# Three 256-column matmuls per weight tile into one PSUM region, and ScalarE as the first reader of PSUM

## What is computed

```
h      = rms_norm(x) * (1 + scale) + shift          # scale, shift, gate: c_act @ mod_w + mod_b
x      = x + gate * mixer(h)                        # attention or Hyena: matmuls with w_in and w_out
h      = rms_norm(x) * (1 + scale2) + shift2
x      = x + gate2 * (square(relu(h @ w1)) @ w2)
```

## Time and profile before

| | |
|---|---|
| median of 3 runs | 2755.25 us (2755.12 to 2758.21) |
| profiled execution, span | 2753.4 us, 41866 instructions |
| HBM read | 597.41 MB, 221 GB/s over the span |
| PE matmuls and weight loads | 13492 each |

### The profile page before, as it was taken

The page is one execution under the profiler, slowest core; times in us unless marked ns, Lnnn a source line. Parts: engine busy times, 40 slices in busy tenths (PEclk is TensorE's granted clock), DMA queues, the critical chain, the costliest instruction groups (busy, mean ns, idle before and its releaser), DMA issues.

```text
span 2753.4 us, 41866 instructions
## 1 busy us (share of the span) xinstructions
PE 2537.7 (92%) x13492; PEld 2107.1 (77%) x13492; DVE 2000.8 (73%) x2357; ACT 1120.8 (41%) x1494; POOL 84.5 (3%) x35
## 2 busy tenths in 40 slices
PE   7879986688999999999989999998899999999996
PEld 2338873376888888888868788787688888888885
DVE  7788658866877878878768788877665555565554
ACT  2234214543444444444434324233344444444442
POOL 0000015500000000000000000000000000000000
PEclk9989988899999999999989999999899999999998
DMA  8858845475888888888848557566466666666662
GB/s 314 321 174 276 285 153 161 160 234 171 271 278 277 282 275 283 276 281 283 277 158 277 195 194 267 175 229 221 153 183 185 188 184 186 187 183 185 188 181 94
DMA packets 441691, 608.73 MB, mean 221 GB/s; under 512 B 18363, under 2 KB 387228, under 8 KB 439580
## 3 DMA queue, kind: packets, MB, share of 16 engines
q1 hardware_dynamic: 440188, 598.53, 66.1%
q10 hardware_dynamic: 1440, 9.44, 0.9%
HBM read 597.41 MB, written 10.49 MB: 221 GB/s over the span
## 4 chain that ended last, share of the span: by engine, by line
PE 84%; DVE 10%; issue 2%; ACT 2%; DMA 1%; DVEq 0%; ACTq 0%; SPq 0%
PE ps L365 49%; PE ps L367 25%; PE ps L1120 2%; PE ps L665 1%; DVE w_lo L397 1%; PE ps L1130 1%; PE ps L937 1%; DMA raw<-in_mod_w 1%; DVE hm L717 1%; DVE hm L725 1%; PE ps L901 1%; DVE sm L1537 1%; DVE lat L731 1%; DVE sm L1534 1%; DVE acc L409 1%
## 5 line engine op out<-in xcount | busy, mean ns | idle before, releaser
L397 DVE TENSOR_TENSOR w_lo<-raw,w_hi 128x1024 fp32r<-128x1024 f32 x720 | 878.5, 1224 | 546.6 <-ACT w_hi L393 542.5
L365 PE MATMUL ps<-lat,w_hi 128*128 128x512 f32 x3200 | 1148.6, 401 | 62.2 <-DVE lat L731 57.0
L393 ACT ACTIVATE w_hi<-raw 128x1024 fp32r<-128x1024 f32 x720 | 760.5, 1060 | 1060.1 <-PE ps L367 987.3
L365 PE MATMUL ps<-alt,w_hi 128*128 128x512 f32 x2688 | 958.9, 400 | 8.5 <-DVE mod L421 5.7
L367 PE MATMUL ps<-lat,w_lo 128*128 128x256 f32 x3200 | 905.9, 283 | 0.0
L365 PEld LDWEIGHTS ps<-lat,w_hi 128*128 128x128 f32 x3200 | 609.8, 191 | 210.2 <-issue 68.4
L367 PE MATMUL ps<-alt,w_lo 128*128 128x256 f32 x2688 | 755.2, 281 | 0.0
L367 PEld LDWEIGHTS ps<-lat,w_lo 128*128 128x128 f32 x3200 | 615.3, 192 | 0.2
L365 PEld LDWEIGHTS ps<-alt,w_hi 128*128 128x128 f32 x2688 | 507.3, 189 | 132.5 <-DVE mod L421 6.0
L367 PEld LDWEIGHTS ps<-alt,w_lo 128*128 128x128 f32 x2688 | 510.1, 190 | 0.3
L409 DVE SCALAR_TENSOR_TENSOR acc<-slab,silu,acc 128x1024 f32<-128x1024 f32 x285 | 367.5, 1293 | 6.1 <-DMA slab<-in_mod_w 2.8
(11 more groups left out here) (185 smaller groups left out, 1519.3 us busy)
## 6 DMA issues: line engine op xcount, KB each, us to landing
raw<-in_mlp_w SPq DMA_DIRECT2D x512, 512.0 KB, 3.7
slab<-in_mod_w SPq DMA_DIRECT2D x336, 512.0 KB, 5.7
raw<-in_hy_w_in SPq DMA_DIRECT2D x96, 512.0 KB, 6.0
raw<-in_mod_w SPq DMA_DIRECT2D x48, 512.0 KB, 6.5
raw<-in_attn_w_in SPq DMA_DIRECT2D x48, 512.0 KB, 6.1
raw<-in_attn_w_out SPq DMA_DIRECT2D x32, 512.0 KB, 5.6
raw<-in_hy_w_out SPq DMA_DIRECT2D x32, 512.0 KB, 5.8
spec_dram<-spec ACTq DMA_DIRECT2D x8, 1024.0 KB, 7.9
```

Source lines behind the costliest of these rows:

```text
L365: e.matmul(ps[:, bank, :], w_hi[:, n % RING, kk, cols], t[:, kb, :], start=(kb == 0), stop=False)
L393: e.activation(w_hi[:, n % RING], raw[:, n % RING], ACT.Copy).then_inc(hi_ready, 1)
L397: e.tensor_tensor(w_lo[:, n % RING], raw[:, n % RING], w_hi[:, n % RING].bitcast(F32), ALU.subtract).then_inc(split_ready, 1)
```

## The change

The two products with `w_hi` become two matmuls of 256 columns, and all three of a tile add into the same 256 columns of PSUM. The halves fb=0 and fb=1 share a bank: g=0 uses bank 0, g=1 bank 1 (the context banks 4 and 5). The first matmul in the bank alone has start set. PSUM then holds the finished sum, so one engine reads it: ACT, with the scale, bias, gate or relu in the same instruction, and then gives `psum_free`. DVE's additions of `lo_sum` go; `lo_sum` and `lo_copied` are removed, and one buffer `gated` [128, 2, 256] serves both g. Readouts:

- `Queries`, `KeysValues`: ACT writes q, keys and values directly; DVE does nothing.
- `Gated`: ACT writes gate times PSUM to `gated`, after a wait on `x_added` for DVE's addition before; DVE does one addition to x.
- `Hidden`: ACT does relu to `sum_sb`, DVE one multiplication.
- `ShortConv`: ACT writes `sum_sb` with its bias; DVE's addition goes.

`act_stats` waits for `x_added`. Two waits of PE ahead of work in other banks grow: `pe_finish` after the output projection waits for the reads of both g, and so does `invert(0, 0)` in the Hyena layer.

```diff
                     kb = (n % 4) * UNIT_KB + kk
                     for fb in range(2):
                         cols = slice(fb * P, (fb + 1) * P)
-                        for t, bank in ((tile, 2 * g + fb), (ctx_tile, 4 + 2 * g + fb)):
+                        for t, bank in ((tile, g), (ctx_tile, 4 + g)):
                             if t is None:
                                 continue
-                            e.matmul(ps[:, bank, :], w_hi[:, n % RING, kk, cols], t[:, kb, :],
-                                     start=(kb == 0), stop=False)
-                            mm = e.matmul(ps[:, bank, 0:TOK], w_lo[:, n % RING, kk, cols], t[:, kb, 0:TOK],
-                                          start=False, stop=(kb == KB - 1))
+                            out = ps[:, bank, fb * TOK:(fb + 1) * TOK]
+                            first, last = (kb == 0 and fb == 0), (kb == KB - 1 and fb == 1)
+                            e.matmul(out, w_hi[:, n % RING, kk, cols], t[:, kb, 0:TOK],
+                                     start=first, stop=False, skip_group_check=True)
+                            e.matmul(out, w_hi[:, n % RING, kk, cols], t[:, kb, TOK:2 * TOK],
+                                     start=False, stop=False, skip_group_check=True)
+                            mm = e.matmul(out, w_lo[:, n % RING, kk, cols], t[:, kb, 0:TOK],
+                                          start=False, stop=last, skip_group_check=True)
                 mm.then_inc(units_done, 1)
         def pe_call(e, T, n, tile, ready, k=None):
...
-            def bank(self, g, part):
-                return ps[:, 2 * g:2 * g + 2, part * TOK:(part + 1) * TOK]
+            def bank(self, g):
+                return ps[:, g, :].rearrange("p (f t) -> p f t", f=2)
             def act_wait(self, e, T, g):
                 e.wait_ge(units_done, 8 * T + 4 * g + 4)
                 e.wait_ge(psum_free, 2 * T + g - 1)
-            def act_head(self, e, T, g):
-                self.act_wait(e, T, g)
-                e.activation(lo_sum[:, g], self.bank(g, 1), ACT.Copy).then_inc(lo_copied, 1)
-
             def act_tail(self, e, T, g):
+                pass
+
+            def dve_head(self, e, T, g):
                 pass
             def dve_tail(self, e, T, g):
...
             def act_head(self, e, T, g):
                 self.act_wait(e, T, g)
-                e.activation(lo_sum[:, g], self.bank(g, 1), ACT.Copy, scale=QSCALE).then_inc(lo_copied, 1)
-
-            def dve_head(self, e, T, g):
-                e.wait_ge(lo_copied, 2 * T + g + 1)
-                e.scalar_tensor_tensor(q[:, ds(4 * self.i + 2 * g, 2), :], self.bank(g, 0), QSCALE, lo_sum[:, g],
-                                       ALU.mult, ALU.add).then_inc(psum_free, 1)
+                e.activation(q[:, ds(4 * self.i + 2 * g, 2), :], self.bank(g), ACT.Copy, scale=QSCALE).then_inc(psum_free, 1)
         class KeysValues(Readout):
             def __init__(self, dst):
                 self.dst = dst
-            def ctx_bank(self, g, part):
-                return ps[:, 4 + 2 * g:6 + 2 * g, part * TOK:(part + 1) * TOK]
-
             def act_head(self, e, T, g):
                 self.act_wait(e, T, g)
-                e.activation(lo_sum[:, g], self.bank(g, 1), ACT.Copy)
-                e.activation(sum_sb[:, g], self.ctx_bank(g, 1), ACT.Copy).then_inc(lo_copied, 1)
-
-            def dve_head(self, e, T, g):
-                e.wait_ge(lo_copied, 2 * T + g + 1)
                 d = self.dst[:, 2 * g:2 * g + 2, :]
-                e.tensor_tensor(d[:, :, 0:TOK], self.bank(g, 0), lo_sum[:, g], ALU.add)
-                e.tensor_tensor(d[:, :, TOK:2 * TOK], self.ctx_bank(g, 0), sum_sb[:, g],
-                                ALU.add).then_inc(psum_free, 1)
+                e.activation(d[:, :, 0:TOK], self.bank(g), ACT.Copy)
+                e.activation(d[:, :, TOK:2 * TOK], self.bank(4 + g), ACT.Copy).then_inc(psum_free, 1)
         class Gated(Readout):
...
             def act_head(self, e, T, g):
                 self.act_wait(e, T, g)
                 e.wait_ge(mod_ready, self.ready)
+
+                e.wait_ge(x_added, self.n_out + 2 * self.i + g)
                 for fb in range(2):
                     f = 4 * self.i + 2 * g + fb
                     bias = gate_bias[:, ds(f, 1)] if self.bias else 0.0
-                    ins = e.activation(lo_sum[:, g, fb], ps[:, 2 * g + fb, TOK:2 * TOK], ACT.Identity,
+                    ins = e.activation(gated[:, fb], ps[:, g, fb * TOK:(fb + 1) * TOK], ACT.Identity,
                                        bias=bias, scale=mod[:, ds(self.gate + f, 1)])
-                ins.then_inc(lo_copied, 1)
+                ins.then_inc(psum_free, 1)
             def dve_head(self, e, T, g):
-                e.wait_ge(lo_copied, 2 * T + g + 1)
-                for fb in range(2):
-                    f = 4 * self.i + 2 * g + fb
-                    xf = x[:, ds(f, 1), :]
-                    ins = e.scalar_tensor_tensor(xf, ps[:, 2 * g + fb:2 * g + fb + 1, 0:TOK],
-                                                 mod[:, ds(self.gate + f, 1)], xf, ALU.mult, ALU.add)
-                ins.then_inc(x_hi_added, 1)
-                e.wait_ge(x_hi_added, self.n_out + 2 * self.i + g + 1)
+                e.wait_ge(psum_free, 2 * T + g + 1)
                 xg = x[:, ds(4 * self.i + 2 * g, 2), :]
-                e.tensor_tensor(xg, xg, lo_sum[:, g], ALU.add).then_inc(psum_free, 1)
+                e.tensor_tensor(xg, xg, gated[:], ALU.add).then_inc(x_added, 1)
         class Hidden(Readout):
...
             def __init__(self, i, n_hid):
                 self.i, self.n = i, n_hid
+            def act_head(self, e, T, g):
+                self.act_wait(e, T, g)
+                e.activation(sum_sb[:, g], self.bank(g), ACT.Relu).then_inc(psum_free, 1)
+
             def dve_head(self, e, T, g):
-                e.wait_ge(lo_copied, 2 * T + g + 1)
-                e.tensor_tensor(sum_sb[:, g], self.bank(g, 0), lo_sum[:, g], ALU.add).then_inc(psum_free, 1)
                 e.wait_ge(psum_free, 2 * T + g + 1)
-                e.scalar_tensor_tensor(sum_sb[:, g], sum_sb[:, g], 0.0, sum_sb[:, g],
-                                       ALU.max, ALU.mult).then_inc(squared, 1)
+                e.tensor_tensor(sum_sb[:, g], sum_sb[:, g], sum_sb[:, g], ALU.mult).then_inc(squared, 1)
             def act_tail(self, e, T, g):
                 e.wait_ge(squared, self.n + 2 * self.i + g + 1)
...
             def act_head(self, e, T, g):
                 self.act_wait(e, T, g)
                 for fb in range(2):
-                    ins = e.activation(lo_sum[:, g, fb], ps[:, 2 * g + fb, TOK:2 * TOK], ACT.Identity,
+                    ins = e.activation(sum_sb[:, g, fb], ps[:, g, fb * TOK:(fb + 1) * TOK], ACT.Identity,
                                        bias=vec("b_in", self.col + 2 * g + fb))
-                ins.then_inc(lo_copied, 1)
-
-            def dve_head(self, e, T, g):
-                e.wait_ge(lo_copied, 2 * T + g + 1)
-                e.tensor_tensor(sum_sb[:, g], self.bank(g, 0), lo_sum[:, g], ALU.add).then_inc(psum_free, 1)
+                ins.then_inc(psum_free, 1)
             def act_tail(self, e, T, g):
                 e.wait_ge(psum_free, 2 * T + g + 1)
...
-        def act_stats(e, k, c, T):
-
-            e.wait_ge(psum_free, 2 * T + 2)
+        def act_stats(e, k, c):
+
+            e.wait_ge(x_added, X_FROM[k] + 2 * c + 2)
             e.wait_ge(square_sums, 4 * k + c)
             e.activation(sq[:, 0], x[:, ds(4 * c, 4), :], ACT.Square).then_inc(squares, 1)
...
             e.wait_ge(mod_ready, FIN_ATT + 2)
             pe_call(e, T_OUT, 4, alt, lambda i: lambda j: (head_ready, 2 + HEADS), 2)
-            e.wait_ge(psum_free, 2 * T_MLP0 - 1)
+            e.wait_ge(psum_free, 2 * T_MLP0)
             e.wait_ge(pool_used, 4 + KB)
             pe_finish(e, M_MLP0, FIN_OUT, 2, acc_pool)
             pe_stats(e, 2, 3)
...
                             (under_first, None, under_last)[k])
                 e.wait_ge(in_back, 16)
-                e.wait_ge(psum_free, 2 * (T_HY + 3 * c + 2) + 1)
+                e.wait_ge(psum_free, 2 * (T_HY + 3 * c + 3))
                 invert(0, 0)
                 invert(0, 1)
                 turn(1, 0)
```

More of the change, by code:

```diff
@@ L159, in build @@
         acc = sb("acc", [P, 2, SLAB])
-        lo_sum = sb("lo_sum", [P, 2, 2, TOK])
+        gated = sb("gated", [P, 2, TOK])
         sum_sb = sb("sum_sb", [P, 2, 2, TOK])
@@ L237, in build @@
         units_done = sem("units_done")
-        lo_copied, psum_free = sem("lo_copied"), sem("psum_free")
+        psum_free = sem("psum_free")
         slabs_used, acc_ready = sem("slabs_used"), sem("acc_ready")
@@ L251, in build @@
         gains, normed, norm_hi, norm_ready = sem("gains"), sem("normed"), sem("norm_hi"), sem("norm_ready")
-        x_hi_added = sem("x_hi_added")
+        x_added = sem("x_added")
```

(10 more changed lines are left out.)

## The result

The changed kernel took 2817.3 us (median of 4, 2812.7 to 2822.3), the kernel before on the same chip 2756.7: ratio 1.0221, interval 1.0197 to 1.0244. It is slower by 60.5 us where 4 us less was forecast, and outside the range. The profiled execution has a span of 2810.1 us against 2753.4, 56.7 more.

The account below looks back on a forecast made before the run. PE was taken as the bound, with everybody waiting for it. From 2755.25 us, -3.2 for the matmuls, zero for the readouts in the calls and -0.8 for stage ends gave 2751.3 us, range 2730 to 2781.

Parts of the forecast that it names:

- The bound: Whole kernel: PE is what everybody waits for; relieving DVE gains nothing in the calls; 1 ns per tile is 5.9 us.
- the division of the 27 ns: Quick-pace tile's time above 320 ns: 6.7 ns per 256 columns, 3.3 ns per matmul; three 256-column slots would take 350 ns.
- The bound above: Upper limit for three 256-column matmuls per tile: 0.120 per slot, 360 ns per tile, +59 us.
- Slots of 0.120 in all units, or a stall in the third addition: Rival for PE's tiles: slots of 0.120, or 3 ns stall adding to the same PSUM columns; 2810 us, chance 0.08.
- A price per matmul, the slow pace kept: Rival for PE's tiles: third matmul adds 3.3 ns in both paces; +19.6 us, 2774 us, chance 0.26.
- All in columns: Rival: price all in columns, slow pace belongs to the 512-column form; all tiles 346.7 ns, 2732 us, chance 0.20.
- The two paces: In the calls: about 300 units at 2.773 us and 420 at 2.827; +8.0 - 11.2 = -3.2 us from the split.
- Part 2: ACT reads PSUM first, with an added wait on `x_added` in `Gated`; zero in the calls.
- Part 3: Ends of stages, where PE stands still: savings and Hyena's added wait sum to -0.8 us.
- Stage ends: Three ends like the layer-0 MLP's lose 0.89 us of L503, 3 x -0.9 = -2.7; output projection -0.8.
- Hyena: First inversion waits for ACT's read of g=1 after the last matmul; +1.0 us each, four times, +4.0.
- the keys and values: DVE's 0.69 and 0.61 us between ACT's reads and PE's transposes go; -1.3 us.

Follow-up runs that it names:

- experiment 1: Kernel before with only the 512-column matmul split into two of 256 writing the two bank halves, readouts unchanged; 2809.1 us against 2758.8, ratio 1.0168.
- experiment 4: Kernel before with matmuls over the two halves fb reordered to 512, 512, 256, 256 columns; 2754.4 us against 2758.8, ratio 0.9977.
- experiment 6: Kernel before with each unit's eight 512-column matmuls first, then its eight of 256; 2755.1 us against 2758.0, ratio 0.9995.
- experiment 2: Kernel before with its matmuls kept but ACT alone reading PSUM, the low product left out of the result; 2752.1 us against 2758.8, ratio 0.9968.
- experiment 5: Second separate kernel of bare fp32r matmul streams: pairs behind six lead-ins, more lengths, narrower weights; pairs took 346.9 or 353.8 ns.
- experiments 3: Separate kernel of bare fp32r matmul streams, other engines idle, against no kernel; 256 columns took 120.0 ns, 512 took 227.0, the pair 353.

## Why the prediction was wrong, point by point

**The bound** was read rightly: relieving DVE by 135.6 us (some 130 forecast) gave nothing in the calls, and 1 ns per tile is worth 5.9 us.

**The step that failed** is the division of the 27 ns. I took the distance from a 256-column start to the next 512-column start, 117 ns, for the price of a 256-column matmul, and had 230 left for the other: "6.7 ns per 256 columns and 3.3 ns per matmul". Streams of one kind give 120.0 and 226.8. Their sum, 346.8, is the quick pace exactly; the sum was right and the parts were each 3.3 ns off in opposite directions. For the old kernel that error cancels. Three of one kind add it up: 3 x 3.3 = 10 ns per tile, x 5888 = 59 us. Put as prices, 320 + 2 x 13.3 = 346.7 and 320 + 3 x 13.3 = 360, against the forecast's 350. The price per matmul is 13.3 ns at 256 columns and 13.5 at 512, not 3.3. Between unlike neighbours the distance between starts isn't the price of the first.

**The bound above** that I gave this term, 0.120 per slot and 2810 us, was the true value. I gave it 0.08 and left it out of the range because the earlier trace rows "show 117": rows rounded to 10 ns, and none of a 256-column matmul behind another. A slot in a succession that no row showed, counted 17664 times, deserved more of the chance and the range.

**The rivals.** "Slots of 0.120 in all units, or a stall in the third addition" came true in its first half; experiment 1 rules out the second. "A price per matmul, the slow pace kept" had the mechanism and a quarter of its size, and the slow pace wasn't kept: three equal matmuls have one pace. "All in columns" was the reverse of what is there.

**The two paces** aren't a property of the 512-column form or of a stage. They belong to the alternation, and what ran ahead turns them. Taking them as fixed to stages gave -3.2 us from a gain and a loss that were both wrong. All calls slow or all quick span 736 x 0.053 = 39 us, and the kernel before ran from 2738 to 2776 us on one chip; that the first explains the second is argued, not shown. For it: ten runs of experiment 4 and twelve of experiment 6, with one pace each, lie within 10 and 12 us, while ten of experiment 2, with both paces, spread over 28. Against it as the only cause: the start and the attention stretch vary by about 10 us each.

**The rule weighed.** The Trainium skill ("TensorE: Matmul & The Clock Gate", Back-to-back issue gap) gives N / 2.4 + 2.5 ns for isolated gaps, by which I had estimated 109.2 and 215.8 ns. I said that the trace agreed with its fixed part in kind. The streams show 120.0 and 226.8, so the measurement decides against it here. It did point the right way, to a price per matmul.

**Part 2** was right at zero in the calls: no wait of ACT on DVE's addition shows. **Part 3** had the right signs and small sizes. Stage ends gave 1.5 to 2.2 us instead of 0.9, as the sums of squares kept part of the full clock in this execution; other executions show that this part comes and goes without the change, so the surplus was not earned by it. Hyena cost 1.25 us per chunk instead of 1.0: 1.10 of waiting, and 0.26 for a slower inversion, less 0.13 in its transposes. The ends together gave -2.3, without the keys and values, for a forecast of -0.8 with them and +0.5 without.

## What to carry to other kernels

Price an operation by a stream of its own kind in the order in which it will run; a distance taken from between unlike neighbours can hide several ns that the next kernel pays thousands of times. When PE is the bound, splitting a 512-column fp32r matmul with 128 weight columns into two of 256 costs 13 ns (2 x 120.0 against 226.8), and into four of 128 it would take 4 x 111.7 = 447 ns, an estimate from the streams; a saving on DVE can't pay for it. A bound of a term that is multiplied by thousands belongs inside the range unless a row excludes it.

## What the runs showed of the hardware that was not expected

- A matmul of 128 to 224 columns takes the same 111.7 ns with full weights of 128 columns; with weights of 64 columns, 128 moving ones take 60.0 (experiment 5).
- The excess over the columns isn't smooth: 13.3 ns at 256, 11.7 at 288, 20.0 at 448, 16.7 at 480, 13.5 at 512 (experiments 3 and 5).
- One and the same alternation of 512 and 256 columns runs at 346.7 or 353.3 ns per pair: in the kernel for hundreds of us with no wait in the trace, and in the bare streams, of 10 to 17 us each, with every other engine idle. Its pace can turn at a few other matmuls in between. By what rule stays open.
- The page of the profile after has 0.67 MB on the instruction queue against 0.49, and all calls hold 2.880 us per unit, so the longer loop body cost nothing that the trace shows.
